# A two-block model on one core: in the second block, attention steps set between the halves of the input units, Fourier and gating steps between later pairs, and one score buffer in place of two

## The reference

```python
px = modulate(rms_norm(x, g1), sh1, sc1) @ w_in      # the same for ctx
qx, kx, vx, fx, ux, gvx = split(px)                   # 8 query heads, 2 key/value heads, 64 wide
qx, kx = rope(rms_norm(qx, q_g)), rope(rms_norm(kx, k_g))
k_all, v_all = concat([kc, kx]), concat([vc, vx])     # 768 keys
mix = concat([attention(qx, k_all, v_all), fourier_mix(fx), chunk_spatial_gate(ux, gvx)]) @ w_out
x = x + gt1 * mix
x = x + gt2 * squared_relu_mlp(modulate(rms_norm(x, g2), sh2, sc2))
```

## Time and profile before

| | us |
|---|---|
| median of three runs (3006.84 to 3011.09) | 3007.17 |
| the profiled execution | 3007.32 |
| its span | 3005.5 |

### The profile page before, as it was taken

The page is one execution under the profiler, slowest core; times in us unless marked ns, Lnnn a source line. Parts: engine busy times, 40 slices in busy tenths (PEclk is TensorE's granted clock), DMA queues, the critical chain, the costliest instruction groups (busy, mean ns, idle before and its releaser), DMA issues. The chain is left out here.

```text
span 3005.5 us, 36673 instructions
## 1 busy us (share of the span) xinstructions
PE 2804.0 (93%) x14298; PEld 2326.8 (77%) x14298; DVE 1704.1 (57%) x2637; ACT 938.5 (31%) x1440; POOL 156.1 (5%) x84
## 2 busy tenths in 40 slices
PE   7898999999999986998988999999999899999999
PEld 7777777877877875776866778888888677878887
DVE  3886666666577878785545455442333546554333
ACT  2212334444232221332334332122122335342222
POOL 0000000000000000000025200000000006200000
PEclk8999999999999998999998999999999999999999
DMA  5242343433245643432300024321222120122332
GB/s 205 91 141 92 99 140 119 137 125 126 93 157 185 194 128 118 135 109 78 123 4 1 25 82 141 119 92 63 64 63 64 48 85 1 38 82 91 98 92 97
DMA packets 88541, 296.33 MB, mean 99 GB/s; under 512 B 10289, under 2 KB 13361, under 8 KB 87857
## 3 DMA queue, kind: packets, MB, share of 16 engines
q1 hardware_dynamic: 88368, 293.98, 30.3%
HBM read 291.85 MB, written 2.10 MB: 98 GB/s over the span
## 5 line engine op out<-in xcount | busy, mean ns | idle before, releaser
L754 PE MATMUL turns<-h_hi,w_hi 128*128 128x512 f32 (+1 forms) x2480 | 800.7, 372 | 62.8 <-ACT u_padded L1124 31.9
L754 PE MATMUL turns<-h_hi,w_lo 128*128 128x512 f32 (+1 forms) x2480 | 780.3, 364 | 0.0
L754 PE MATMUL turns<-h_lo,w_hi 128*128 128x512 f32 (+1 forms) x2480 | 777.9, 363 | 0.0
L754 PEld LDWEIGHTS turns<-h_hi,w_hi 128*128 128x128 f32 x2480 | 424.6, 192 | 163.8 <-issue 64.8
L754 PEld LDWEIGHTS turns<-h_lo,w_hi 128*128 128x128 f32 x2480 | 422.0, 192 | 73.3 <-issue 1.0
L754 PEld LDWEIGHTS turns<-h_hi,w_lo 128*128 128x128 f32 x2480 | 420.6, 191 | 75.1
L1199 DVE TENSOR_TENSOR w_lo<-w_raw,w_hi 128x1024 fp32r<-128x1024 f32 x300 | 366.9, 1223 | 140.8 <-ACT w_hi L995 138.4
L995 ACT ACTIVATE w_hi<-w_raw 128x1024 fp32r<-128x1024 f32 x300 | 315.7, 1053 | 377.5 <-PE turns L754 354.7
L709 POOL TENSOR_SCALAR tmp<-tmp,softmax_stats 128x768 f32<-128x768 f32 (+1 forms) x80 | 155.9, 1951 | 2428.8 <-DVE softmax_stats L1427 2428.4
L1202 DVE SCALAR_TENSOR_TENSOR x_lat<-turns,modulation,x_lat 128x512 f32<-128x512 f32 x112 | 84.1, 751 | 336.9 <-PE turns L754 336.9
L754 PE MATMUL turns<-m_hi,w_lo 128*128 128x512 f32 (+1 forms) x768 | 233.2, 358 | 0.0
(11 more groups left out here) (212 smaller groups left out, 3405.2 us busy)
## 6 DMA issues: line engine op xcount, KB each, us to landing
w_raw<-in_wpack SPq DMA_DIRECT2D x300, 512.0 KB, 3.5
ada_raw<-in_adapack SPq DMA_DIRECT2D x176, 512.0 KB, 4.0
bias<-in_bias SPq DMA_DIRECT2D x64, 320.0 KB, 3.0
ada_first_a<-in_adapack SPq DMA_DIRECT2D x12, 512.0 KB, 8.7
x_lat<-in_xT SPq DMA_DIRECT2D x1, 2048.0 KB, 8.5
x_ctx<-in_ctxT SPq DMA_DIRECT2D x2, 1024.0 KB, 8.6
ada_first_b<-in_adapack SPq DMA_DIRECT2D x4, 512.0 KB, 14.7
cond_rows<-in_crow SPq DMA_DIRECT2D x4, 512.0 KB, 10.3
```

Source lines behind the costliest of these rows:

```text
L754: ins = pe.matmul(dst[:, lo:lo + sz], w, x[:, lo:lo + sz], start=first and n == 0, stop=last and n == 2)
```

## The change

It is in the second block alone (a flag `na=True` on the first block's `vtrans` keeps its V tiles apart from the second block's). It does this:

1. Only key, first query unit and value stand ahead of attention. The other eight units, in the order su0, sq2, su1, sq3, sf0, sgv0, sf1, sgv1, are each cut in halves, and the first half stands in the even, the second in the odd step of the attention pairs 0 to 7; unit sq1's second half stands just ahead. The weight pack is reordered in the same way.
2. The head norms of these units stand in the pairs 0, 2, 4, 6 and 8: the sums ahead of the unit's first half in the even step, `back` and `rope` or `gnorm` behind the unit in the odd step. Their sums and transposes take turns, with no filler ahead; query units 1 to 3 use `GV` for their temporaries.
3. Gating and Fourier steps (`gtrans`, `spgate` with `gsplit`, twice; `four1`, `four2`, twice) stand one behind each attention step of pairs 9 to 12.
4. All scores use score buffer 0, one step ahead of the transposes (it was two steps and two buffers). Transposes use score buffer 1 and not a turn. The V product takes a turn of its own.
5. Explicit table loads on ScalarE ahead of roots and after them in the gating units are gone. Tiles get other places: the attention output goes to `SQh`/`SQl` (the source "S" of the output projection), exponentials to `EXB`, V to `V2h`/`V2l`.

```diff
-        for j, (e, m, t) in enumerate(units):
-            if j < 2:
-                u = full("H", e, t, m, after=tiles, layer=L, what=e)
...
-            else:
-                first = half_unit("H", e, t, 0, m=m)
-                if todo is not None:
-                    hn_of[todo.what, todo.m] = head_steps(todo)
...
+        sk = full("H", "sk", TT, 0, after=tiles, layer=L, what="sk")
+        head_scale(sk, head_sums(sk, False), False)
+        sq = {0: full("H", "sq", T, 0, after=tiles, layer=L, what="sq")}
+        join(sk, sq[0])
+        first_half("v")
+        head_scale(sq[0], head_sums(sq[0], False), False)
+        v = second_half("v")
+        first_half("sq", 1)
+        vt = add("vtrans")
+        vt.after = [v]
...
+                sc[n] = add("scores", na=False, pair=m, half=half, qt=qt, st=0, eb=n % 2, nk=nk)
+                sc[n].after = [hn_of["sq", m]]
...
-            soft[n].scores, soft[n].trans = sc.get(n + 2), tr.get(n)
+            soft[n].scores, soft[n].trans = sc.get(n + 1), tr.get(n)
...
-            mm = add("pvmm", nk=todo[n][3])
-            mm.pt = n // 2 % 2
+            mm = add("pvmm", nk=todo[n][3], has_turn=True)
+            mm.pt = 1
...
+        s_scores(0)
+        s_soft(-1)
+        sq[1] = second_half("sq", 1)
+        units = {0: ("su", 0), 1: ("sq", 2), 2: ("su", 1), 3: ("sq", 3), 4: ("sf", 0), 5: ("sgv", 0), 6: ("sf", 1), 7: ("sgv", 1)}
+        heads = {0: ("sq", 1), 2: ("sq", 2), 4: ("sq", 3), 6: ("sgv", 0), 8: ("sgv", 1)}
+        rest_of = [(f, m) for m in range(2) for f in (gtrans, spgate)] + [(f, m) for m in range(2) for f in (four1, four2)]
+        made_of = {("sq", 1): sq[1]}
         for n in range(len(todo)):
 
-            s_scores(n + 2)
-            if n % 2 == 0 and n >= 4:
-                s_pv(n - 4).in_turn = True
-            tr[n] = add("trans", na=False, eb=n % 2, col=n % 2 * P, nk=todo[n][3], has_turn=True, qt=todo[n][2])
...
+            j = n // 2
+            s_scores(n + 1)
+            if n % 2 == 0 and n:
+                mm = s_pv(n - 2)
+            tr[n] = add("trans", na=False, eb=n % 2, col=n % 2 * P, nk=todo[n][3], qt=todo[n][2])
+            tr[n].pt, tr[n].after = 1, [soft[n - 1]]
+            if n % 2 == 0 and j in heads:
+                hn = head_sums(made_of[heads[j]], True)
+            if n % 2 == 0 and j in units:
+                first_half(*units[j])
             s_soft(n)
...
+            if n % 2 == 0 and n:
+                s_pv_out(n - 2, mm)
+            if n % 2 and j in units:
+                last_in = made_of[units[j]] = second_half(*units[j])
+            if n % 2 and j in heads:
+                head_scale(made_of[heads[j]], hn, True)
+            if j > 8 and rest_of:
+                f, m = rest_of.pop(0)
+                f(m)
...
                     give(act.activation(RMS[:, 0:n], src[:, 0:n], ACT.Sqrt, bias=EPSC[:], scale=1.0 / 64))
-                    if s.what == "sgv":
-                        load_table(ACT.Exp if s.m else ACT.Tanh)
...
-                        if s.ev == "sgv":
-                            load_table(ACT.Sqrt)
```

More of the change, by code:

```diff
@@ L331, in plan @@
[L331 to L367, removed]
+        hn_of = {}
@@ new lines, in head_sums, with head_scale @@
+        def head_sums(u, turn):
+            hn = add("hnorm", T=u.T, what=u.what, m=u.m, layer=L, st=0, has_turn=turn)
+            hn.after, hn.own = [u], u.own
+            return hn
+        def head_scale(u, hn, turn):
+            back = add("back", T=u.T, has_turn=turn)
+            back.after = [hn]
+            if u.what == "sgv":
+                back.reader = add("gnorm", T=u.T, m=u.m, layer=L)
+            else:
+                back.reader = add("rope", T=u.T, what=u.what, m=u.m, layer=L, st=1)
+            back.reader.back, back.reader.own = back, u.own
+            hn_of[u.what, u.m] = back.reader
@@ new lines, in first_half, with second_half @@
+        def first_half(e, m=0):
+            half_unit("H", e, TT if e == "v" else T, 0, m=m)
+        def second_half(e, m=0):
+            u = half_unit("H", e, TT if e == "v" else T, 1, m=m, layer=L, what=e, pair=0)
+            u.own = e == "sq" and m > 0
+            with_ada(u)
+            return u
+        sk = full("H", "sk", TT, 0, after=tiles, layer=L, what="sk")
+        head_scale(sk, head_sums(sk, False), False)
+        sq = {0: full("H", "sq", T, 0, after=tiles, layer=L, what="sq")}
@@ L424, in plan, with gtrans, spgate @@
-        for n in (len(todo) - 4, len(todo) - 2):
-            mm = s_pv(n)
-            mm.has_turn = True
-            s_pv_out(n, mm)
+        nts = T // P
+        gt, gsp, mix, ab = {}, {}, {}, {}
+        def gtrans(m):
+            gt[m] = add("gtrans", T=T, m=m, has_turn=True)
+            gt[m].after = [hn_of["sgv", m]]
+        def spgate(m):
+            for n0 in range(0, nts, 4):
+                add("spgate", T=T, m=m, n0=n0, nn=min(4, nts - n0), layer=L, has_turn=True).after = [gt[m]]
+            gsp[m] = add("gsplit", T=T, m=m)
@@ new lines, in four1, with four2 @@
+        def four1(m):
+            ab[m] = [add("four1", m=m, n0=n0, nn=min(4, nts - n0), has_turn=True, in_end=last_in) for n0 in range(0, nts, 4)]
+        def four2(m):
+            mix[m] = add("four2", m=m, T=T, has_turn=True)
+            mix[m].after = ab[m]
+        s_scores(0)
[3 more added lines that the diff above has]
+        heads = {0: ("sq", 1), 2: ("sq", 2), 4: ("sq", 3), 6: ("sgv", 0), 8: ("sgv", 1)}
@@ L428, in plan @@
+        assert not rest_of
+        s_pv_out(len(todo) - 2, s_pv(len(todo) - 2))
         ready = [pv_of[0], pv_of[1], pv_of[2], pv_of[3], mix[0], mix[1], gsp[0], gsp[1]]
         for m in range(KT):
-            full("H", "xupd", T, m, after=ready if m == 0 else (), sect=sect + 2, nxT=T, late=m == 0)
+            full("S", "xupd", T, m, after=ready if m == 0 else (), sect=sect + 2, nxT=T, late=m == 0)
         tiles = norm(T, 6 + L, sect + 3)
@@ L466, in plan @@
     for s in steps:
-        n = {"hnorm": 0, "back": 0, "rope": 1, "vtrans": 1, "scores": s.st, "trans": 1 if s.na else None}.get(s.kind)
-        if n is not None:
+        n = {"hnorm": 0, "back": 0, "rope": 1, "vtrans": 1, "scores": s.st, "trans": 1}.get(s.kind)
+        if n is not None and not s.has_turn:
             fills[n] += 1
```

216 lines of the change are left out of this document (94 added, 122 removed).

## The result

The changed kernel takes **3203.99 us** (median of 4 runs, 3199.99 to 3211.84) beside 3009.13 us for the kernel before on the same chip: a ratio of **1.065, 95% interval 1.0624 to 1.0676**. It is slower, as forecast. It is outside the likeliest case's own one (3110 to 3195) and at the foot of the rival *deeper clock loss or a costlier switch of tables* (3200 to 3240). The profiled execution took 3211.84 us, with a span of 3210.0.

A forecast was written before the change was run, and what follows sets the result against it. TensorE was taken to bound both layers of the second block, busy 87% and 92%. From 3007.3 us, +50 and +41 for the layers at full clock and +47 for lost clock gave 3145 us, range 3070 to 3205.

The forecast's parts named there:

- likeliest case: Whole kernel: the forecast itself, 3145 us, with its own range 3110 to 3195 us; chance 0.60.
- deeper clock loss or a costlier switch of tables: Rival: TensorE's clock falls further, or ScalarE's table switches cost more, giving 3200 to 3240 us; chance 0.07.
- bare odd step: Uncovered attention steps with one score buffer: odd 5.3 us, even 6.3, so a pair takes 11.6 instead of 6.42.
- run of six: Six bare steps, four over six key tiles and two over two: 29.6 us for 21.06.
- Wait (a): Even steps of pairs 2, 4, 6: the unit's first half waits 5.2 us for the V product's eviction.
- wait (b): Pair after a head: the unit's first half waits for VectorE's rope, 6 to 7 us, second layer 3 to 5.
- the weave runs at TensorE's pace: Rival: evictions and rope arrive in time, only bare steps are dearer, 2980 us; chance 0.07.
- half cover: Rival: waits in the woven and gating pairs are half as long, 3040 to 3070 us; chance 0.07.
- 3007 + 91 + 47: Whole kernel: time before, plus 50 and 41 us for the two layers at full clock, plus 47 for lost clock.
- full-clock sum: Second block's layers with waits but no extra clock loss: 414 us for 364.2, and 289.6 for 248.5.
- four terms: Lost clock: 15 and 8 us in the two layers' woven stretches, 18 and 6 in the rest.
- The rest of the kernel: First block and both MLPs: within 1 us of the time before.

The follow-up runs named there:

- e9_clock_all: The changed kernel with the fillers of e5_clock_short and more of them at head sums and transposes where the clock still fell: 3146.01 us, ratio 1.0459.
- e5_clock_short: The changed kernel with constant filler matmuls in TensorE's waits at the heads and in the pairs from 13 on: 3157.25 us, ratio 1.0476.

## Why the prediction was right or wrong

**The sign and its mechanisms were right.** A bare odd step was summed as 5.3 and an even one as 6.3; at a clock of 1.00 they take 5.21 (1738.23 - 1733.02) and 6.40 (1744.63 - 1738.23), and the run of six 30.24 for 29.6. In the changed kernel itself, where the prediction looked for these distances, the low clock makes them longer. Wait (a) is in pairs 2, 4 and 6, wait (b) in pairs 1, 3 and 5. The rivals *the weave runs at TensorE's pace* and *half cover* fell by the idle time alone: pairs 0 to 7 idle 185.80 - 135.74 = 50.1 us and 153.50 - 118.06 = 35.4 us, for 53 and 32 in the prediction. That these totals agree is partly luck, since the single waits in them do not.

**Single steps were off.** Wait (a) was summed as 5.2 us and is 7.1 on average. I had let the root's table load hide; it stands behind ScalarE's wait for the sums, 1.28 us. VectorE's maximum (0.96 in the timeline above) was not in the sum either: the exponential's load starts 0.07 us after it. That is 42.7 - 6 x 5.2 = 11.5 us over six waits. Wait (b) had about the right size (6.2 for 6 to 7 in the first layer, 2.6 for 3 to 5 in the second) at the wrong instruction: I looked for the reader of the turn, and score buffer 1 has the same reader and is needed earlier. The table loads stand where I put them, ahead of root and exponential. The Trainium skill (ScalarE: Activation LUTs, What ACT_TABLE_LOAD costs) adds a drain of about 1380 ns to each load. Here the root starts 1.30 us after its load's start and the exponential 1.30 after its own, so no drain stands behind either load. Ahead of both ScalarE idles, but in the earlier trace rows no idle time stands ahead of the load, so that row has no room for a drain on either side.

**The step that failed is the last addition, 3007 + 91 + 47.** The full-clock sum (sum), the kernel with the clock held (held, e9_clock_all) and the changed kernel (after), in us. The last two are cut at GpSimd's scalings as above, the sum goes by pairs of steps:

| stretch | sum | held | after |
|---|---|---|---|
| first layer, entry | 59.5 | 61.8 | 61.7 |
| pairs 0 to 7 | 168 | 175.6 | 185.8 |
| pair 8 to the projection | 186 | 204.5 | 232.5 |
| second layer, entry | 47.6 | 50.8 | 49.1 |
| pairs 0 to 7 | 133 | 149.2 | 153.5 |
| pair 8 to the projection | 109 | 116.1 | 129.0 |

Over both layers: sum 703, held 758, after 812. The changed kernel is 108 us above the full-clock sum, and I had allowed 47 for the clock.

- **The clock** is worth at least 812 - 758 = 54 us (58 by the medians, 3204 - 3146), and more by what the fillers overran and by what the clock still lacked (0.94 to 0.98 behind the entries, but for the 1.00 of the second layer's bare part). It was guessed well as a level: 0.83 and 0.75 in the prediction, 0.81, 0.76 and 0.68 in the first layer, 0.82, 0.83 and 0.70 in the second. What was too small was the price of the level. In the bare part, where e5_clock_short shows both ends, 141.7 us at 0.68 became 117.3 at 1.00: 24.4 us, or 0.54 of the 0.32 x 141.7 = 45 us that the clock withheld. In the second layer it is 50.7 - 41.7 = 9.0 us of 15, or 0.59. I had charged 18 of 46 us, a share of 0.39, in the first layer's rest and 6 of 27, or 0.22, in the second's. The prediction names TensorE's work as 70% of the woven stretch and 54% of the bare one, but its four terms use smaller shares, for which it gives no row; with 0.70 and 0.54 they are 20 + 25 + 16 + 15 = 76 us and not 47. The Trainium skill (TensorE: Matmul & The Clock Gate, HAM oscillation) warned of a clock lost again and again between waits. The trace agrees: 0.68 where TensorE is busy 65% of the time (91.64 of 141.70), against 0.81 where it is busy 73%.
- **The chain** is up to 758 - 703 = 55 us longer than summed. 11.5 of them are wait (a). In the table 18.5 us stand between pair 8 and the projection of the first layer, and 16.2 in the woven pairs of the second. The first are hardly in the bare steps: from step 28 on e5_clock_short takes 98.5 us for the sum's 96.4. One wait is the scores' wait for the softmax in pair 8 (5.4 and 6.5 us in the waits above), where no unit is left to cover the gating input's norm. How the rest divides between my sums and fillers that outlasted their waits stays open.

So of the rival that the time fell to, the costlier switch of tables did not happen, and the deeper clock did only in part: no stretch went to 0.59.

The two errors have the same sign. I followed the steps pair by pair with each engine at its best, and rounded the waits down to what I could name.

**The rest of the kernel** was to stay within 1 us. It grew by 5.6: the first layer starts 2.8 us later (1341.5 for 1338.7), and the stretch between the two layers is 2.2 longer, whose first 23.5 us have a clock of 0.90 for 1.00 before. The 2.8 need no cause: the first block is the same in all these kernels, and the layer starts anywhere from 1330.1 us (e9_clock_all) to 1341.5.

**What the change is made of**, as the runs undo it: the single buffer in the bare pairs 74 us, the sums behind the V product 30, the split ahead of the rope 17; 73 remain, which these runs do not tell apart. Each of these includes the clock that the wait costs: in the bare pairs e5_clock_short gives back 24.4 + 9.0 = 33 us by clock alone.

## What to carry to other kernels

Before you interleave two streams of work, list for every buffer its last reader, and find where that reader stands in its own engine's queue: the large waits of the woven stretches here (the V product's eviction behind a softmax, transposes and sums behind a rope) are of that kind, and two of the three fell on another instruction than the one I had looked at. A buffer given up to make room for an interleave is paid in every step that the interleave does not cover: here 22 and 6 bare steps at the end of the layers cost 74 us, where the heads' waits that the weave was to hide were summed at 12 us a layer. And charge the clock on top of the waits. In the bare stretches here, where TensorE waits a third of the time, 0.54 and 0.59 of what the clock withheld were lost in time; in the first layer's pairs 0 to 7, where it waits a quarter, at least 10 of 30 us.

## What the hardware showed that I had not expected

A constant fp32 matmul of 128 x 256 stands in the profile as two records 0.23 us apart, so ten of them fill 4.5 us and not 2.3. The trace of the kernel before has it already: its two fillers at a head are four records. Wait (a) does not get shorter with the clock. In e5_clock_short's second layer, with the clock at 1.00, its timeline reads:

```profile
2516.43 4.56 PE L863 MATMUL turns<-dft,ones 128*128 128x256 f32 x20
2523.75 0.47 PE L756 MATMUL turns<-h_hi,w_hi 128*128 128x512 f32 x1 [2.75 <-DVE sq_lo L1209]
```

From the fillers' start behind the sums to the unit's first half it is 7.3 us, for 7.2 without fillers at a clock of 0.82: the wait is ScalarE's and VectorE's, and only TensorE's own work between the waits gets shorter.
